# A post-norm trunk on one core: which of a norm's eight feature tiles are turned before the next projection, and when its tiles are normalised

## The chip, the cores and the metric

One core of a Trainium2 chip runs the whole program. The metric is the device time of one execution in microseconds (us); the median of three runs is compared with that of another kernel on the same chip. Engines: TensorE (PE; PEld is its weight load), VectorE (DVE), ScalarE (ACT), GpSimd (POOL) and SyncE (SP, which here only starts transfers). Each engine works through its own queue in order and waits on semaphores for the others.

## What is computed

x is 512 rows of 1024 features. The trunk has two layers, all in float32:

```
for layer in range(2):
    mix = _even_mixer(x, ...) if layer % 2 == 0 else _odd_mixer(x, ...)
    x = _layer_norm(ALPHA * x + mix, ln1_g[layer], ln1_b[layer])
    x = _layer_norm(ALPHA * x + _swiglu(x, gate, up, down), ln2_g[layer], ln2_b[layer])
```

The even mixer is one input projection, gated linear attention and windowed softmax attention, and one output projection; the odd one is a gated DeltaNet between two projections. So there are four norms: norm 1 after the even mixer, norm 2 after the first feed-forward part, norm 3 after the odd mixer, norm 4 at the end. Only norms 1 to 3 are followed by another projection.

## The kernel before

**Products.** A float32 product is made of three passes of rounded parts: high x high, low x high and high x low (`mm3`, L1663). Weights come in blocks of 1 MB into two slots of `w_raw`; ACT rounds each half of a block to `w_hi` (`split_to`, L807) and POOL subtracts to get `w_lo` (L681). Activations are kept by feature, `x_hi` and `x_lo`, 8 feature tiles of 128 x 512.

**A norm** sits between two projections. The sublayer's output comes row-wise, four tiles t of 128 rows, in two halves of 512 columns. The last weight block of the second half runs tile by tile (`tm_group` with `in_turn`), so its banks fill one after another. DVE adds each filled bank to `x_tm` (L1237), takes statistics (L1239) and aggregates them (L1219); ACT takes the square root (L841); DVE takes the reciprocal (L1194) and normalises both halves (L1210). `layer_norm` on DVE (L1190) normalises tile t-1 after the aggregate of tile t, and tile 3 last; in norm 4 it normalises tile t directly (L1221).

PE then turns the rows to features: `turn_x` (L1834), 4 row tiles x 8 feature tiles = 32 transposes of 128 x 128, tile by tile, into eight banks `xT`; feature k is complete with row tile 3. `round_x` on ACT (L819) and DVE (L1159) applies scale and bias to each feature and makes `x_hi` and `x_lo`; feature 1 goes by DVE (`f_ab`) and an ACT copy. Then `fm_block` with `fresh` (L1688) runs the next projection's first block, two output banks, as features arrive: two high passes per feature and bank (L1696, L1697), and the pass with `x_lo` (L1709) two features later. It issues features 0 and 1 bank by bank, 48 products in all. ACT queues the split of the block behind that one (both pieces) between `layer_norm` and `round_x`. POOL splits the low part of its first piece once all is normalised, and of its second once the last `x_lo` is there (L778 to L781).

**Banks.** `unit_plan` (L178) lists all uses of the eight PSUM banks in PE's order and hands them out from a ring; the swap at L277 puts feature 1's bank ahead of feature 0's for the next unit.

**Way in.** While the first weights and features land, PE runs 16 products on zeros (L1879). Then `tm_group` of `sq` runs, three passes each; its first product waits for the low parts of weight and feature tile 0, which DVE makes (L1258, L1261) from ACT's high parts (L883, L879).

**Query copies.** In the even mixer PE turns queries and keys, ACT copies the banks to `s_qT` and `s_kT` (L915, L917), and the bank of query tile 0 is the one that the next product, `a2` (L1904), fills. ACT splits the second block of `gv` ahead of these copies (L911).

Of the kernel before, what the change touches and what calls it, by code (L numbers as in the profile page):

```python
# [164 lines left out]

EVEN_FILLERS = [[("gr", t)] for t in range(NT)]
# [11 lines left out]
def unit_plan():  # L178
# [4 lines left out]
    def ln(i):  # L183
        u.extend(("xT", i, k) for k in range(KD))

    def ffn(layer):
        for f in range(0, KF, 2):
            u.extend([("gate", layer, f), ("gate", layer, f + 1), ("up", layer, f), ("up", layer, f + 1)])
        for half in range(2):
            u.extend(("down", layer, half, t) for t in tiles)  # L190
# [18 lines left out]
    for i, n in enumerate(CONV_ORDER):  # L209
        u.append(("conv", n))  # L210
        if i == 1:
            u.append(("ba_fm",))
# [39 lines left out]
    for key in u:  # L252
# [24 lines left out]
        if key[0] == "xT" and key[2] == KD - 1:  # L277
            a = turn % len(ring)
            c = (turn + 1) % len(ring)
            ring[a], ring[c] = ring[c], ring[a]  # L280
# [6 lines left out]
def trunk_kernel(nc, A, out):  # L287
# [8 lines left out]
    with ctx:  # L296
# [202 lines left out]
        def low_weights_all(e, b):  # L499

            low_weights(e, b, len(pieces(b)) - 1)
# [295 lines left out]
        def _(act):  # L797
# [21 lines left out]
            def round_x(i):  # L819
# [7 lines left out]
                for k in range(2, KD):  # L827
# [10 lines left out]
            def layer_norm(i):  # L838
                for t in range(NT):
                    act.wait_ge(s["ln_var"], NT * (i - 1) + t + 1)  # L840
# [70 lines left out]
            split_to(first_block[("gv",)] + 1)  # L911

            for t in range(NT):
                full(act, ("qT", t))
# [64 lines left out]
            layer_norm(1)  # L979
            split_to(first_block[("gate", 0, 0)] + 1)  # L980
            round_x(1)
# [3 lines left out]
            layer_norm(2)  # L985
            split_to(first_block[("conv", KD)] + 1)
# [5 lines left out]
            round_x(2)  # L992
# [137 lines left out]
            layer_norm(3)  # L1130
            split_to(first_block[("gate", 1, 0)] + 1)
            round_x(3)
# [6 lines left out]
        def _(dve):  # L1139
# [50 lines left out]
            def layer_norm(i, group, layer):  # L1190
# [22 lines left out]
                for half in range(2):  # L1213
                    for t in range(NT):
                        if (group, layer, half, t) not in FILLED:
                            add_sublayer(i, group, layer, half, t)
                        if half:
# [3 lines left out]
                            if i == 4:  # L1221
                                normalise(t)
                            elif t:
                                normalise(t - 1)
                if i < 4:
                    normalise(NT - 1)
# [425 lines left out]
        def _(pe):  # L1652
# [35 lines left out]
            def fm_block(b, keys, fresh=None, width=P):  # L1688
# [10 lines left out]
                for k in range(KD) if fresh is not None else ():  # L1699
                    for n in range(len(keys)):  # L1700
                        if k == 0:
                            high(0, n)
                            high(1, n)
                        elif k > 1:
                            high(k, n)
# [530 lines left out]
```

## Time and profile before

| | |
|---|---|
| median of 3 runs | 1243.77 us (1243.36 to 1244.42) |
| the profiled execution, its own time | 1243.55 us |
| its span in the trace | 1241.7 us, so 1.85 us lie around it |
| PE busy | 1227.7 us, 99% |
| DVE, ACT, POOL busy | 436.9, 450.6, 587.9 us |
| granted TensorE clock, mean | 0.998 |

The page says that PE is busy nearly always, so time can come only from work taken off PE or from the few stretches where it waits. The timeline of one engine lists its instructions with the idle time before them and what ended it; the list of waits sums that by line and releaser.

### The profile page before, as it was taken

To read this page: it belongs to the slowest core of one execution; us is meant where nothing else is said; L and a number is where in the kernel's file an instruction comes from. 1 tells how busy PE (TensorE), PEld (TensorE's weight loads), DVE (VectorE), ACT (ScalarE), POOL (GpSimd) and SP (SyncE) were. 2 spreads that over 40 slices of the span, in tenths; PEclk is the share of its full clock that TensorE was granted. 3 is DMA by queue.
4 is the path that set the end of the run, shared out by engine and by line. 5 is a ranking of instruction groups with operands and counts; after the bars stand their busy time and mean duration, and the time that the engine had idled before them with its cause. 6 is when DMAs were issued, how large, how long until landed. Compare 5 with 4: busy or idle time off the path is not lost.

```text
span 1241.7 us, 17153 instructions
## 1 busy us (share of the span) xinstructions
PE 1227.7 (99%) x7112; PEld 1012.4 (82%) x7112; DVE 436.9 (35%) x772; ACT 450.6 (36%) x670; POOL 587.9 (47%) x280
## 2 busy tenths in 40 slices
PE   9999999999999999999999999999999999999997
PEld 7878887888888888887777889888788888888885
DVE  4556526201011100127678845654511111110105
ACT  4167825232223221225544455542532233221211
POOL 4244444943444343445744347444684444435341
PEclk9999999999999999999999999999999999999999
DMA  9321052333322333232353342124233222324231
GB/s 321 96 69 69 3 169 69 102 102 102 99 93 80 98 124 118 102 102 60 92 123 116 91 114 94 27 69 136 68 102 102 92 92 88 102 85 146 75 102 68
DMA packets 106064, 122.96 MB, mean 99 GB/s; under 512 B 18946, under 2 KB 80580, under 8 KB 105988
## 3 DMA queue, kind: packets, MB, share of 16 engines
q1 hardware_dynamic: 98244, 118.56, 29.9%
q10 hardware_dynamic: 7744, 3.32, 1.1%
q8 instruction: 56, 0.92, 0.3%
q14 instruction: 20, 0.16, 0.0%
HBM read 117.93 MB, written 3.70 MB: 98 GB/s over the span
## 4 chain that ended last, share of the span: by engine, by line
PE 95%; DVE 3%; DVEq 0%; ACT 0%; issue 0%; ACTq 0%
PE bank L1665 27%; PE bank L1666 27%; PE bank L1667 27%; PE bank L2088 4%; PE bank L1696 1%; PE bank L1697 1%; PE bank L1709 1%; DVE stats L1239 1%; DVE x_tm L1237 1%; PE bank L1919 1%; PE bank L2197 1%; PE bank L1731 1%; PE bank L2034 1%; PE bank L2180 0%; PE bank L1855 0%; DVE x_tm L1200 0%
## 5 line engine op out<-in xcount | busy, mean ns | idle before, releaser
L681 POOL TENSOR_TENSOR w_lo<-w_raw,w_hi 128x1024 fp32r<-128x1024 f32 (+1 forms) x200 | 470.2, 2373 | 546.9 <-ACT w_hi L816 521.8
L1665 PE MATMUL bank<-x_hi,w_hi 128*128 128x512 f32 x880 | 344.3, 391 | 0.0
L1666 PE MATMUL bank<-x_lo,w_hi 128*128 128x512 f32 x880 | 342.5, 389 | 0.0
L1667 PE MATMUL bank<-x_hi,w_lo 128*128 128x512 f32 x880 | 342.5, 389 | 0.0
L816 ACT ACTIVATE w_hi<-w_raw 128x1024 fp32r<-128x1024 f32 (+1 forms) x200 | 196.4, 1032 | 206.5 <-issue 161.2
L1665 PEld LDWEIGHTS bank<-x_hi,w_hi 128*128 128x128 f32 x880 | 165.2, 188 | 35.4 <-issue 0.8
L1667 PEld LDWEIGHTS bank<-x_hi,w_lo 128*128 128x128 f32 x880 | 165.2, 188 | 34.4
L1666 PEld LDWEIGHTS bank<-x_lo,w_hi 128*128 128x128 f32 x880 | 165.2, 188 | 33.7
L1246 DVE TENSOR_TENSOR f_ab<-bank,f_ab 128x512 f32<-128x512 f32 x44 | 30.4, 692 | 364.7 <-PE bank L1667 364.7
L1667 PE MATMUL bank<-w_hi,h_lo 128*128 128x512 f32 x352 | 136.9, 389 | 0.0
L1665 PE MATMUL bank<-w_hi,h_hi 128*128 128x512 f32 x352 | 136.9, 389 | 0.0
L1666 PE MATMUL bank<-w_lo,h_hi 128*128 128x512 f32 x352 | 136.9, 389 | 0.0
L1665 PE MATMUL bank<-w_hi,x_hi 128*128 128x512 f32 (+1 forms) x288 | 112.2, 390 | 0.0
L1667 PE MATMUL bank<-w_hi,x_lo 128*128 128x512 f32 (+1 forms) x288 | 109.0, 378 | 0.0
L1666 PE MATMUL bank<-w_lo,x_hi 128*128 128x512 f32 (+1 forms) x288 | 108.9, 378 | 0.0
L1237 DVE SCALAR_TENSOR_TENSOR x_tm<-x_tm,bank 128x512 f32<-128x512 f32 x32 | 22.0, 688 | 246.3 <-PE bank L1667 238.7
L864 ACT ACTIVATE h_hi<-f_ab 128x512 fp32r<-128x512 f32 x44 | 27.8, 632 | 187.4 <-DVE f_ab L1246 187.4
L859 ACT ACTIVATE f_ab<-bank 128x512 f32<-128x512 f32 x44 | 26.3, 598 | 144.8 <-PE bank L1667 140.5
L1667 PEld LDWEIGHTS bank<-w_hi,h_lo 128*128 128x128 f32 x352 | 66.1, 188 | 13.8
L1665 PEld LDWEIGHTS bank<-w_hi,h_hi 128*128 128x128 f32 x352 | 66.1, 188 | 13.7
L1666 PEld LDWEIGHTS bank<-w_lo,h_hi 128*128 128x128 f32 x352 | 66.1, 188 | 13.7
L1454 DVE SCALAR_TENSOR_TENSOR KH<-bank,convw,KH 128x511 f32<-128x511 f32 (+2 forms) x72 | 53.9, 749 | 28.8 <-ACT KH L1004 25.9
(291 smaller groups left out, 1252.1 us busy)
## 6 DMA issues: line engine op xcount, KB each, us to landing
w_raw<-ffn_w_gate_dram SPq DMA_DIRECT2D x22, 1024.0 KB, 5.3
w_raw<-ffn_w_up_dram SPq DMA_DIRECT2D x22, 1024.0 KB, 5.3
w_raw<-ffn_w_down_dram SPq DMA_DIRECT2D x20, 1024.0 KB, 5.0
w_raw<-od_w_in_dram SPq DMA_DIRECT2D x16, 1024.0 KB, 5.8
w_raw<-ev_w_in_dram SPq DMA_DIRECT2D x8, 1024.0 KB, 5.6
w_raw<-ev_w_out_dram SPq DMA_DIRECT2D x4, 1024.0 KB, 5.1
w_raw<-od_w_out_dram SPq DMA_DIRECT2D x4, 1024.0 KB, 5.1
x_fm<-x_fm_dram SPq DMA_DIRECT2D x8, 256.0 KB, 6.9
```

What stands on the lines that cost most here:

```text
L681: pool.tensor_tensor(w_lo[:, b % 2, c], w_raw[:, b % 2, c], w_hi[:, b % 2, c].bitcast(F32), ALU.subtract).then_inc(w_lo_ready, 1)
L816: act.activation(w_hi[:, i % 2, c], w_raw[:, i % 2, c], ACT.Copy).then_inc(w_hi_ready, 1)
L859: take(act.activation(f_ab[:, j, :], bank(("gate", layer, f + j))[:, :], ACT.Silu), ("gate", layer, f + j))
L864: act.activation(h_hi[:, f + j, :], f_ab[:, 2 + j, :], ACT.Copy).then_inc(s["h_hi_ready"], 1)
L1237: take(dve.scalar_tensor_tensor(cols, cols, ALPHA, bank(key)[:, :], ALU.mult, ALU.add), key)
L1239: dve.bn_stats(stats[:, t, half, :], cols).then_inc(s["half_stats"], 1)
L1246: take(dve.tensor_tensor(f_ab[:, 2 + f % 2, :], bank(("up", layer, f))[:, :], f_ab[:, f % 2, :], ALU.mult), ("up", layer, f))
L1454: ins = dve.scalar_tensor_tensor(dst, bank(key)[:, 0:SEQ - back], convw[:, tap:tap + 1], dst, ALU.mult, ALU.add)
L1665: pe.matmul(out_ap, st[0], mv_[0], start=start, stop=False)
L1666: pe.matmul(out_ap, st[0], mv_[1], start=False, stop=False)
L1667: return pe.matmul(out_ap, st[1], mv_[0], start=False, stop=stop)
L2088: return pe.matmul(o, a, b_, start=True, stop=True)
```

## The change

- `turn_x` turns features 0 to 5 (`NOW = 6`) of the four row tiles before the projection, and features 6 and 7 behind its third feature, k == 2. The bank plan follows, and the swaps of ring positions go. `fm_block` issues features 0 and 1 like the others, both banks of a feature together.
- DVE normalises each tile right behind its aggregate in all norms.
- ACT splits the first piece of the following block ahead of the square root of tile 3, and its second piece at the end of `round_x` (`split_part`). In norm 2 three transfers that ACT starts, `ba_w`, `o_upto` and `o_negt`, come behind `round_x`.
- Way in: 12 products on zeros, then four high x high products that wait only for the high parts, then the passes with low parts of weight row 0, then the rest.
- ACT splits `gv`'s second block behind the copies of query and key tiles 0 and 1.

```
--- before.py
+++ after.py
@@ -163,6 +163,7 @@
            (1, 1): ("og", 1, 0), (1, 3): ("og", 1, 1), (2, 1): ("og", 1, 2), (2, 3): ("og", 1, 3),
            (3, 1): ("mix", 1, 0, 0), (3, 3): ("mix", 1, 0, 1)}
 
+NOW = 6
 EVEN_FILLERS = [[("gr", t)] for t in range(NT)]
 TAIL_FILLERS = {0: [("mix", 0, 0, 0), ("mix", 0, 0, 1)], 1: [("mix", 1, 0, 2)]}
 LAST_FILLERS = {0: [("mix", 0, 0, 2)], 1: []}
@@ -180,12 +181,15 @@
     u = []
     tiles = range(NT)
 
-    def ln(i):
-        u.extend(("xT", i, k) for k in range(KD))
+    def ln(i, features=range(NOW)):
+        u.extend(("xT", i, k) for k in features)
 
     def ffn(layer):
         for f in range(0, KF, 2):
-            u.extend([("gate", layer, f), ("gate", layer, f + 1), ("up", layer, f), ("up", layer, f + 1)])
+            u.extend([("gate", layer, f), ("gate", layer, f + 1)])
+            if f == 0:
+                ln(2 * layer + 1, range(NOW, KD))
+            u.extend([("up", layer, f), ("up", layer, f + 1)])
         for half in range(2):
             u.extend(("down", layer, half, t) for t in tiles)
 
@@ -209,6 +213,7 @@
     for i, n in enumerate(CONV_ORDER):
         u.append(("conv", n))
         if i == 1:
+            ln(2, range(NOW, KD))
             u.append(("ba_fm",))
         if i == 2:
             u.append(("ba",))
@@ -274,10 +279,6 @@
         else:
             b = ring[turn % len(ring)]
             turn += 1
-        if key[0] == "xT" and key[2] == KD - 1:
-            a = turn % len(ring)
-            c = (turn + 1) % len(ring)
-            ring[a], ring[c] = ring[c], ring[a]
         order[b] = len(slots)
         slots[key] = (b, uses[b])
         uses[b] += 1
@@ -816,7 +817,17 @@
                         act.activation(w_hi[:, i % 2, c], w_raw[:, i % 2, c], ACT.Copy).then_inc(w_hi_ready, 1)
                     split[0] += 1
 
-            def round_x(i):
+            def split_part(b, j):
+
+                assert split[0] == b
+                if j == 0:
+                    act.wait_ge(w_landed[b % 2], 16 * (b // 2 + b % 2))
+                    act.wait_ge(*block_end[b - 2])
+                    low_weights_all(act, b - 2)
+                act.activation(w_hi[:, b % 2, pieces(b)[j]], w_raw[:, b % 2, pieces(b)[j]], ACT.Copy).then_inc(w_hi_ready, 1)
+                split[0] += j
+
+            def round_x(i, b):
 
                 gcol = 32 * ((i + 1) % 2) + 8 * ((i - 1) // 2)
                 full(act, ("xT", i, 0))
@@ -834,9 +845,12 @@
                             low_part_there(act, i, k - 4)
                         take(act.activation(f_ab[:, k % 4, :], bank(("xT", i, k))[:, :], ACT.Identity, scale=scale,
                                             bias=bias), ("xT", i, k))
-
-            def layer_norm(i):
+                split_part(b, 1)
+
+            def layer_norm(i, b=None):
                 for t in range(NT):
+                    if t == NT - 1 and b is not None:
+                        split_part(b, 0)
                     act.wait_ge(s["ln_var"], NT * (i - 1) + t + 1)
                     act.activation(rstd[:, t:t + 1], mv[:, t, 1:2], ACT.Sqrt, bias=eps[:, 0:1])\
                        .then_inc(s["ln_stat"], 1)
@@ -908,9 +922,10 @@
             split_to(first_block[("gv",)])
             full(act, ("ga",))
             take(act.activation(g_ga[:, :], bank(("ga",))[:, :], ACT.Copy), ("ga",))
-            split_to(first_block[("gv",)] + 1)
 
             for t in range(NT):
+                if t == 2:
+                    split_to(first_block[("gv",)] + 1)
                 full(act, ("qT", t))
                 take(act.activation(s_qT[:, :, tile_cols[t]], fm4(("qT", t)), ACT.Copy), ("qT", t))
                 full(act, ("kT", t))
@@ -976,20 +991,18 @@
             split_to(first_block[("mix", 0, 1)])
             full(act, ("mix", 0, 0, NT - 1))
             split_to(first_block[("gate", 0, 0)])
-            layer_norm(1)
-            split_to(first_block[("gate", 0, 0)] + 1)
-            round_x(1)
+            layer_norm(1, first_block[("gate", 0, 0)] + 1)
+            round_x(1, first_block[("gate", 0, 0)] + 1)
 
             ffn(0)
             split_to(first_block[("conv", KD)])
-            layer_norm(2)
-            split_to(first_block[("conv", KD)] + 1)
+            layer_norm(2, first_block[("conv", KD)] + 1)
+            round_x(2, first_block[("conv", KD)] + 1)
 
             act.dma_start(ba_w[:, :, :], A["od_w_in"][0][:, BA0:BA0 + SB].rearrange("(k p) n -> p k n", p=P))\
                .then_inc(s["ba_landed"], 16)
             for dst, c0, n in ((o_upto, 0, P), (o_negt, P, P)):
                 act.dma_start(dst[:, :], A["c_odd"][:, c0:c0 + n]).then_inc(consts, 16)
-            round_x(2)
 
 
             def silu_conv(i):
@@ -1127,9 +1140,8 @@
             split_to(first_block[("mix", 1, 1)])
             full(act, ("mix", 1, 0, NT - 1))
             split_to(first_block[("gate", 1, 0)])
-            layer_norm(3)
-            split_to(first_block[("gate", 1, 0)] + 1)
-            round_x(3)
+            layer_norm(3, first_block[("gate", 1, 0)] + 1)
+            round_x(3, first_block[("gate", 1, 0)] + 1)
             ffn(1)
             split_to(NB - 1)
             layer_norm(4)
@@ -1218,12 +1230,7 @@
                             dve.wait_ge(s["half_stats"], 2 * NT * (i - 1) + NT + t + 1)
                             dve.bn_aggr(mv[:, t, :], stats[:, t, :, :].rearrange("p a b -> p (a b)"))\
                                .then_inc(s["ln_var"], 1)
-                            if i == 4:
-                                normalise(t)
-                            elif t:
-                                normalise(t - 1)
-                if i < 4:
-                    normalise(NT - 1)
+                            normalise(t)
 
             def add_sublayer(i, group, layer, half, t):
 
@@ -1698,11 +1705,9 @@
 
                 for k in range(KD) if fresh is not None else ():
                     for n in range(len(keys)):
-                        if k == 0:
-                            high(0, n)
-                            high(1, n)
-                        elif k > 1:
-                            high(k, n)
+                        high(k, n)
+                    if k == 2:
+                        turn_x(fresh, range(NOW, KD))
                     for kl in [k - 2] * (k > 1) + [KD - 2, KD - 1] * (k == KD - 1):
                         low_part_there(pe, fresh, kl)
                         for n in range(len(keys)):
@@ -1733,7 +1738,7 @@
                                         skip_group_check=True)
                 done(ins, key)
 
-            def tm_group(name, wait_k, src=xcols, kt=KD, in_turn=False, tiles=range(NT), pair_last=False, late=0):
+            def tm_group(name, wait_k, src=xcols, kt=KD, in_turn=False, tiles=range(NT), pair_last=False, late=0, begun=0):
 
 
                 b = first_block[name]
@@ -1759,7 +1764,7 @@
                         for t in tiles:
                             pe.matmul(bank((*name, t))[:, 0:width], src(kk, tile_cols[t])[0], weights(b, kk, 0, width)[1],
                                       start=False, stop=False)
-                    for kk, t in [(kk, t) for kk, t in steps if kk >= late or k0]:
+                    for kk, t in [(kk, t) for kk, t in steps if kk >= max(late, begun) or k0]:
                         if kk > waited:
                             weights_there(b, kk)
                             wait_k(k0 + kk)
@@ -1831,10 +1836,10 @@
                 if (t, place) in FILLERS:
                     tile_of(FILLERS[t, place], k0, k1)
 
-            def turn_x(i):
+            def turn_x(i, features=range(NOW)):
 
                 for t in range(NT):
-                    for k in range(KD):
+                    for k in features:
                         if k % 4 == 0:
                             pe.wait_ge(s["z_norm"], 2 * (NT * (i - 1) + t) + k // 4 + 1)
                         ps = fill(("xT", i, k)) if t == 0 else bank(("xT", i, k))
@@ -1875,9 +1880,18 @@
                              pair_last=(layer, half) == (1, 1))
 
             pe.wait_ge(s["warm_ready"], 1)
-            for _ in range(16):
+            for _ in range(12):
                 pe.matmul(bank(("skv", NT - 1))[:, :], warm[:, 0:P], warm[:, :], start=True, stop=True)
-            tm_group(("sq",), lambda k: low_part_there(pe, 0, k))
+            pe.wait_ge(s["w_first_hi"], 1)
+            pe.wait_ge(s["x_hi_ready"], 1)
+            for t in range(NT):
+                pe.matmul(fill(("sq", t))[:, :], x_hi[:, 0, tile_cols[t]], weights(0, 0, 0, 512)[0], start=True, stop=False)
+            weights_there(0, 0)
+            low_part_there(pe, 0, 0)
+            for t in range(NT):
+                pe.matmul(bank(("sq", t))[:, :], x_lo[:, 0, tile_cols[t]], weights(0, 0, 0, 512)[0], start=False, stop=False)
+                pe.matmul(bank(("sq", t))[:, :], x_hi[:, 0, tile_cols[t]], weights(0, 0, 0, 512)[1], start=False, stop=False)
+            tm_group(("sq",), lambda k: low_part_there(pe, 0, k), begun=1)
             tm_group(("skv",), no_wait)
             pe.wait_ge(s["eye_landed"], 16)
             pe.wait_ge(consts, 16 * N_CONST)
```

## Rows read from the trace of the kernel before

**Rows 1.** The page, busy time of each engine, share of the span, instructions.

```profile
PE 1227.7 (99%) x7112; PEld 1012.4 (82%) x7112; DVE 436.9 (35%) x772; ACT 450.6 (36%) x670; POOL 587.9 (47%) x280
```

**Rows 2.** Waits of PE: waiting line, releaser: us in total, times, longest.

```profile
PE bank L1841 <- DVE x_tm L1210: 1.1, 3, 0.4
PE bank L1696 <- DVE f_ab L1176: 0.7, 2, 0.3
PE bank L1841 <- DVE x_tm L1237: 0.6, 3, 0.2
PE bank L1904 <- ACT s_qT L915: 0.6, 1, 0.6
```

**Rows 3.** Timeline of PE, norm 1: start, duration, line, operation, count, idle before.

```profile
193.73 0.93 PE L1841 MATMUL bank<-eye,x_tm 128*128 128x128 f32 x7
...
196.44 2.23 PE L1841 MATMUL bank<-eye,x_tm 128*128 128x128 f32 x16 [0.38 <-DVE x_tm L1210]
199.00 0.47 PE L1696 MATMUL bank<-x_hi,w_hi 128*128 128x512 f32 x1 [0.34 <-DVE f_ab L1176]
...
208.77 1.52 PE L1709 MATMUL bank<-x_lo,w_hi 128*128 128x512 f32 x6
210.13 0.39 PE L1665 MATMUL bank<-x_hi,w_hi 128*128 128x512 f32 x1
```

**Rows 4.** Timeline of DVE, norm 1.

```profile
185.76 0.69 DVE L1237 SCALAR_TENSOR_TENSOR x_tm<-x_tm,bank 128x512 f32<-128x512 f32 x1 [12.18 <-PE bank L1667]
...
194.11 0.69 DVE L1237 SCALAR_TENSOR_TENSOR x_tm<-x_tm,bank 128x512 f32<-128x512 f32 x1
...
196.95 1.00 DVE L1210 TENSOR_SCALAR x_tm<-x_tm,mv,rstd 128x512 f32<-128x512 f32 x2
198.05 0.81 DVE L1176 TENSOR_SCALAR f_ab<-bank,lnc 128x512 f32<-128x512 f32 x1
```

**Rows 5.** Timeline of ACT, norm 1.

```profile
196.01 1.99 ACT L816 ACTIVATE w_hi<-w_raw 128x1024 fp32r<-128x1024 f32 x2
198.08 0.78 ACT L823 ACTIVATE x_hi<-bank,lnc 128x512 fp32r<-128x512 f32 x1
```

**Rows 6.** Timeline of DVE, norm 4, which normalises each tile at once.

```profile
1219.09 0.69 DVE L1237 SCALAR_TENSOR_TENSOR x_tm<-x_tm,bank 128x512 f32<-128x512 f32 x1 [42.34 <-PE bank L1667]
...
1221.12 0.16 DVE L1194 RECIPROCAL rstd<-rstd 128x1 f32<-128x1 f32 x1 [0.36 <-ACT rstd L841]
1221.32 1.42 DVE L1200 SCALAR_TENSOR_TENSOR x_tm<-x_tm,mv,ln_rows 128x512 f32<-128x512 f32 x2
```

**Rows 7.** Two transposing groups between products in the even mixer, timeline of PE.

```profile
108.58 1.04 PE L1928 MATMUL bank<-eye,s_p 128*128 128x128 f32 x8
109.49 0.66 PE L1855 MATMUL bank<-eye,o_tm 128*128 128x128 f32 x4
```

**Rows 8.** Way in: PE's line 1879 (ns min/median/max, first and last start).

```profile
L1879 PE MATMUL bank<-warm x16: 388/440/796, 1.5 to 6.5; 128*128 128x512 f32 x16
```

**Rows 9.** Way in: timeline of ACT, high part of feature tile 0.

```profile
5.39 0.62 ACT L879 ACTIVATE x_hi<-x_fm 128x512 fp32r<-128x512 f32 x1
```

**Rows 10.** Way in: timeline of DVE, low part of feature tile 0.

```profile
6.13 0.69 DVE L1261 TENSOR_TENSOR x_lo<-x_fm,x_hi 128x512 fp32r<-128x512 f32 x1
```

**Rows 11.** Way in: timeline of PE, first product of sq.

```profile
6.96 0.47 PE L1665 MATMUL bank<-w_hi,x_hi 128*128 128x512 f32 x1
```

**Rows 12.** Query copies: timeline of ACT.

```profile
66.61 2.00 ACT L816 ACTIVATE w_hi<-w_raw 128x1024 fp32r<-128x1024 f32 x2
68.69 0.60 ACT L915 ACTIVATE s_qT<-bank 128x512 f32<-128x512 f32 x1
```

**Rows 13.** Norm 2: last work of round_x on ACT, timeline.

```profile
570.50 0.77 ACT L835 ACTIVATE f_ab<-bank,lnc 128x512 f32<-128x512 f32 x1
```

**Rows 14.** Norm 2: DMA issues, KB and us to landing.

```profile
ba_w<-od_w_in_dram ACTq DMA_DIRECT2D x1, 128.0 KB, 2.7
```

**Rows 15.** Norm 2: timeline of PE, first use of ba_w.

```profile
574.83 1.92 PE L1731 MATMUL bank<-x_hi,ba_w 128*32 128x512 f32 x16
```

More of the change, by code:

```diff
@@ L181, in unit_plan, with ln @@
     tiles = range(NT)
-    def ln(i):
-        u.extend(("xT", i, k) for k in range(KD))
+    def ln(i, features=range(NOW)):
+        u.extend(("xT", i, k) for k in features)
     def ffn(layer):
         for f in range(0, KF, 2):
-            u.extend([("gate", layer, f), ("gate", layer, f + 1), ("up", layer, f), ("up", layer, f + 1)])
+            u.extend([("gate", layer, f), ("gate", layer, f + 1)])
+            if f == 0:
+                ln(2 * layer + 1, range(NOW, KD))
+            u.extend([("up", layer, f), ("up", layer, f + 1)])
         for half in range(2):
@@ L1734, in few_columns, with tm_group @@
                 done(ins, key)
-            def tm_group(name, wait_k, src=xcols, kt=KD, in_turn=False, tiles=range(NT), pair_last=False, late=0):
+            def tm_group(name, wait_k, src=xcols, kt=KD, in_turn=False, tiles=range(NT), pair_last=False, late=0, begun=0):
                 b = first_block[name]
@@ L1761, in tm_group @@
                                       start=False, stop=False)
-                    for kk, t in [(kk, t) for kk, t in steps if kk >= late or k0]:
+                    for kk, t in [(kk, t) for kk, t in steps if kk >= max(late, begun) or k0]:
                         if kk > waited:
@@ L1832, in filler, with turn_x @@
                     tile_of(FILLERS[t, place], k0, k1)
-            def turn_x(i):
+            def turn_x(i, features=range(NOW)):
                 for t in range(NT):
-                    for k in range(KD):
+                    for k in features:
                         if k % 4 == 0:
@@ L1877, in _ @@
             pe.wait_ge(s["warm_ready"], 1)
-            for _ in range(16):
+            for _ in range(12):
                 pe.matmul(bank(("skv", NT - 1))[:, :], warm[:, 0:P], warm[:, :], start=True, stop=True)
-            tm_group(("sq",), lambda k: low_part_there(pe, 0, k))
+            pe.wait_ge(s["w_first_hi"], 1)
+            pe.wait_ge(s["x_hi_ready"], 1)
+            for t in range(NT):
+                pe.matmul(fill(("sq", t))[:, :], x_hi[:, 0, tile_cols[t]], weights(0, 0, 0, 512)[0], start=True, stop=False)
+            weights_there(0, 0)
+            low_part_there(pe, 0, 0)
+            for t in range(NT):
+                pe.matmul(bank(("sq", t))[:, :], x_lo[:, 0, tile_cols[t]], weights(0, 0, 0, 512)[0], start=False, stop=False)
+                pe.matmul(bank(("sq", t))[:, :], x_hi[:, 0, tile_cols[t]], weights(0, 0, 0, 512)[1], start=False, stop=False)
+            tm_group(("sq",), lambda k: low_part_there(pe, 0, k), begun=1)
             tm_group(("skv",), no_wait)
```

54 lines of the change are left out of this document (27 added, 27 removed).

## Prediction

> **What bounds the kernel now.** I read the page first: PE is busy 99% of the span, every other engine half of it or less [rows 1]. So only two things can move the time: work added to or taken from PE, and PE's waits. The list of PE's waits comes next [rows 2]. Two of its lines belong to the transposes of the norms (1.1 and 0.6 us in three norms), one to the first products behind them (0.7 us in two norms, 0.34 in the row of norm 1), and one to the query copies (0.6). That is (1.1 + 0.6) / 3 + 0.34 = 0.9 us of waiting in each of norms 1 to 3 and 0.6 in the even mixer. What the change can remove is therefore about 3 us and a little at the start, and what it adds to PE's path counts in full, because everything behind each norm is PE-bound.
>
> Then the timelines of norm 1, engine by engine [rows 3 to 5]. PE leaves the last sublayer product at 193.73, turns 32 tiles, and begins the projection at 199.00; the 48 products of that first block end at 210.13. Six products take 1.36 us there (208.77 to 210.13), 0.227 each, so 48 need 10.88 and the block's 11.13 hold only 0.25 of waiting. Who ends the wait before 199.00? DVE normalises row tile 3 from 196.95 to 198.05, ACT is busy with a weight split from 196.01 and rounds feature 0 at 198.08 for 0.78, and PE starts 0.14 after that. So PE waits for row tile 3. While it waits it does transposes that cost nothing; the reader should see that 5.3 us of transposes and waits stand before the first product, and that PE isn't what sets their end.
>
> **Tiles normalised at once.** In the kernel before, DVE takes tile t-1 while ACT takes the square root of tile t, so the round trip to ACT is hidden. Norm 4 shows the other order in this same trace [rows 6]: from the add to the start of the normalising 1221.32 - 1219.09 = 2.23 us, with 0.36 idle for ACT's square root in it. From the start of a normalising pair to DVE's next instruction it is 1.10 (196.95 to 198.05) [rows 4]. One row tile thus takes 3.33 us of DVE, in order and with nothing to fill the wait. PE delivers a row tile in 12 products, 2.72 us [rows 3]. DVE falls behind by 0.6 a tile: tile 0 is added at 185.76 as before, tile 3 at 185.76 + 3 x 3.33 = 195.75 in place of 194.11 [rows 4], and its normalising starts at 195.75 + 2.23 = 197.98 in place of 196.95. That is **1.03 us later**, though tiles 0 to 2 are earlier, which nobody needs.
>
> **The split moved.** ACT's first piece (half of 1.99 [rows 5]) now follows the end of PE's last sublayer product at 193.7 or the square root of tile 2, whichever is later, and is done near 195.5. The square root of tile 3 is asked for at about 197.4, so it hides. If the weights landed 2 us late it would cost the excess. The second piece comes behind the last feature; the next block's second half is read some 3 us after the first block ends, and ACT and POOL need 1 and 2.4 us, so I cost it at nothing. What the move gives: feature 0 no longer queues behind the split. Before, half of tile 3 was normalised about 0.6 after 196.95, one transpose takes 0.3 more, and ACT could have begun near 197.85 instead of 198.08.
>
> **First product.** Tile 3's first half is there at 197.98 + 0.6 = 198.58; a transpose 0.3; ACT 0.78; PE 0.14 later [rows 5]: 199.80, against 199.00. So **+0.80** in norm 1. Feature 1 (DVE free at 199.08, 0.81 for f_ab [rows 4], then ACT's copy, no longer than 0.78) is ready near 200.7, when PE has finished the four products of feature 0. It costs at most 0.2.
>
> **Two feature tiles turned later.** Eight transposes leave the stretch where PE waited anyway and enter the stretch where it has no wait to fill. Of the same shape, eight take 0.91 between products (108.58 to 109.49) [rows 7]; the nearest other row gives 2.23 for sixteen, 1.1 for eight, with waits in it [rows 3]. I take **+0.91**. Their banks are those of features 0 and 1, free once DVE has read them near 200.7, and PE gets there at about 202.6, so no wait. The swap of ring positions that falls served a start in feature 1's bank; the two output banks now are those of the last two sublayer tiles, free after DVE's adds, before 197. Cost nothing.
>
> One norm: 0.80 + 0.91 = **1.71**. From below I allow 1.2 (part of the block's 0.25 filled, a shorter chain), from above 2.2 (1.1 for the transposes, the 0.2 for feature 1, a slow first product). Norms 2 and 3 show the same waits in the list [rows 2], so three make 5.13 (3.6 to 6.6).
>
> In norm 2 ba_w now leaves behind round_x. That ends near 570.50 + 0.77 [rows 13] + 1.0 for the delay, the split adds 1.0, the landing 2.7 [rows 14]: 576.0. PE asks at 574.83 [rows 15] + 1.7 = 576.5. Half a microsecond of cover; I cost it at nothing and put the risk (up to 1) into the range.
>
> **Way in.** The sixteen zero products run from 1.5 to 6.75; the last starts at 6.5 [rows 8]. The first real one starts at 6.96, just behind the low part of feature 0, which ends at 6.82 [rows 10, 11]. Without four, at 0.227 each, the warm products end near 5.9. The high part is there at 5.39 + 0.62 = 6.01 [rows 9], so real products start at about 6.14, and after four of them (0.9) the low part has long been there. Everything moves ahead by 6.96 - 6.14 = **0.82** (0 to 0.9: nothing, if a later weight piece of the first blocks takes over).
>
> **Query copies.** The 2.00 us split stands right ahead of the first query copy at 68.69, for which a2 waits 0.61 [rows 2, 12]. Behind two tiles of copies it blocks only banks that the gv products reach 3 us later. **-0.61** (0 to -0.61).
>
> **Sum.** 5.13 - 0.82 - 0.61 = +3.7 us. The span goes from 1241.7 to 1245.4, the profiled execution from 1243.55 to 1247.25; the median of the runs lies 0.22 above that execution, so 1243.77 becomes about **1247.4**. With all bounds: 3.6 - 0.9 - 0.6 = +2.1 and 6.6 - 0 - 0.3 = +6.3, so 1245.9 to 1250.1.
>
> **Rivals.**
> 1. *It does what it is shaped for; faster.* PE's waits in the norms vanish, because feature 0 no longer stands behind the split and the eight transposes fill gaps in the block: 3 x 0.93 + 1.43 = 4.2, 1239.6. For it: the split at 196.01 is really in the way [rows 5]. Against it: only 0.25 of gaps per block, and tile 3 isn't earlier. It decides at the first product of norm 1: at 199.00 - 0.91 = 198.1 or earlier, the norm gains. Chance 0.12.
> 2. *DVE keeps up.* If the round trip of the square root were hidden, tile 3 would be added at 194.11 and normalised 2.23 later, at 196.34; 0.6 ahead and 0.2 by the moved split nearly pay the 0.91. A norm costs 0.1, the whole is -1.1: 1242.7, no difference that can be told. Against it: the 0.36 idle in norm 4 [rows 6]. Chance 0.11.
> 3. *The clock falls.* PE would stand idle about 2.5 us before tile 3, where the longest wait in a norm was 0.4 [rows 2], and four warm products are gone. In the warm-up sixteen products took 5.25 us, against 16 x 0.227 = 3.63 at the 2.4 GHz pace [rows 3, 8]: a restart from 1.2 GHz costs 1.6. Three of them: 1247.4 + 4.9 = 1252.3. Against it: after 5.3 us with no product but transposes and waits, the products at 199.00 went at full pace. Chance 0.07.
>
> The Trainium skill (TensorE: Matmul & The Clock Gate, Part 1: The HAM clock gate) says that a PE found idle is put back to 1.2 GHz, and that page's Part 4, PE-mode transpose, says that transposes don't count as busy in the same way. By these two together the norms of the kernel before should already have lost the clock, and the pace behind 199.00 says that they didn't; the rule speaks against the change, and rival 3 is what it would make of it.
>
> **How the numbers follow.** The forecast case (1245.9 to 1250.1) has 0.70; 0.05 of that ends under 1246.3. I call 0.2%, 2.5 us, the least that a measurement of this kernel tells from no change. Slower by more: 0.65 + 0.07 = 0.72. Within: 0.05 + 0.10 of rival 2 = 0.15. Faster: 0.12 + 0.01 = 0.13. The range takes in the forecast case and rival 2, 1242.5 to 1250.1, and leaves out rivals 1 and 3, 0.19.
>
> **What would show it.** In the trace after: in norms 1 to 3 DVE idles 0.36 before each reciprocal and the adds are 3.3 apart; normalising of tile 3 starts 1.0 later against PE's last sublayer product; PE idles about 2.5 before tile 3's transposes; the first product comes 6.1 behind the last sublayer product, not 5.3; eight transposes of 0.9 stand in the block, which takes 12.0; the first real product is at 6.1; the wait at a2 is gone. Wrong would be the forecast if adds were 2.8 apart, if the block took 11.3 in spite of the transposes, or if products behind the norm were 0.43 apart.

## The result: slower by 0.9%, and the profile after

The changed kernel takes 1255.41 us in the median of four runs (1254.1 to 1256.21), the kernel before 1243.78 on the same chip: a ratio of 1.0092, with a 95% interval of 1.0079 to 1.0105. The forecast was 1247.4 with a range of 1242.5 to 1250.1. Slower was right, the size was not: +11.6 us where +3.7 was forecast. The profiled execution took 1255.61, its span 1253.8 is 12.1 longer than before.

The list of PE's waits of the changed kernel, the counterpart of [rows 2]:

```profile
PE bank L1846 <- DVE x_tm L1222: 9.6, 6, 2.4
PE bank L1884 <- DVE warm L1259: 1.5, 1, 1.5
PE bank L1672 <- POOL w_lo L682: 0.7, 1, 0.7
```

PE now waits 3.2 us a norm for DVE's normalising (line 1222, which was 1210), up to 2.4 at once. The wait at the query copies is gone, and a wait of 0.7 for POOL's low weights has come. The difference between these waits and those of [rows 2] explains some 7 us of 12, so PE must also be slower at work. The timeline of PE in norm 1, against [rows 3]:

```profile
193.22 1.47 PE L1846 MATMUL bank<-eye,x_tm 128*128 128x128 f32 x12
195.46 0.90 PE L1846 MATMUL bank<-eye,x_tm 128*128 128x128 f32 x6 [0.77 <-DVE x_tm L1222]
198.77 0.89 PE L1846 MATMUL bank<-eye,x_tm 128*128 128x128 f32 x6 [2.42 <-DVE x_tm L1222]
200.01 0.47 PE L1703 MATMUL bank<-x_hi,w_hi 128*128 128x512 f32 x1 [0.35 <-issue]
...
201.27 0.63 PE L1703 MATMUL bank<-x_hi,w_hi 128*128 128x512 f32 x1
201.69 0.63 PE L1704 MATMUL bank<-x_hi,w_lo 128*128 128x512 f32 x1
202.12 0.63 PE L1703 MATMUL bank<-x_hi,w_hi 128*128 128x512 f32 x1
...
203.83 0.53 PE L1703 MATMUL bank<-x_hi,w_hi 128*128 128x512 f32 x1
...
204.42 1.04 PE L1846 MATMUL bank<-eye,x_tm 128*128 128x128 f32 x8
205.22 0.71 PE L1714 MATMUL bank<-x_lo,w_hi 128*128 128x512 f32 x2
...
213.47 0.39 PE L1672 MATMUL bank<-x_hi,w_hi 128*128 128x512 f32 x1
```

Read the starts, not only the durations: from 201.27 to 203.83 there are six steps from product to product, 0.427 us each, where they were 0.227 apart before. I call a product slow when the next one starts more than 0.4 behind it: seven in norm 1, nine in norm 2 and nine in norm 3. 512 columns in 0.427 us are 1.2 GHz, the lower of the two levels. The granted clock says the same: in norm 1 it is 1.00 up to 200.5, 0.50 from 201.0 to 204.0 and 1.00 again from 204.5, and its mean over the span is 0.991 against 0.998. What PE did before it: transposes, and idle for 0.77 and 2.42 us. In norm 2 the clock falls earlier, near 566.0 and still inside the wait, so there the transposes of tile 3 are slow too:

```profile
567.20 1.54 PE L1846 MATMUL bank<-eye,x_tm 128*128 128x128 f32 x6 [2.42 <-DVE x_tm L1222]
```

Six take 1.54 where the six at 198.77 took 0.89. This is rival 3.

DVE in norm 1, against [rows 4]:

```profile
185.25 0.69 DVE L1244 SCALAR_TENSOR_TENSOR x_tm<-x_tm,bank 128x512 f32<-128x512 f32 x1 [12.18 <-PE bank L1674]
...
187.27 0.17 DVE L1206 RECIPROCAL rstd<-rstd 128x1 f32<-128x1 f32 x1 [0.36 <-ACT rstd L855]
187.47 1.75 DVE L1222 TENSOR_SCALAR x_tm<-x_tm,mv,rstd 128x512 f32<-128x512 f32 x2
189.32 0.69 DVE L1244 SCALAR_TENSOR_TENSOR x_tm<-x_tm,bank 128x512 f32<-128x512 f32 x1
...
192.63 0.69 DVE L1244 SCALAR_TENSOR_TENSOR x_tm<-x_tm,bank 128x512 f32<-128x512 f32 x1
...
195.95 0.69 DVE L1244 SCALAR_TENSOR_TENSOR x_tm<-x_tm,bank 128x512 f32<-128x512 f32 x1
...
198.17 1.00 DVE L1222 TENSOR_SCALAR x_tm<-x_tm,mv,rstd 128x512 f32<-128x512 f32 x2
```

The adds of tiles 1, 2 and 3 are 3.31 and 3.32 apart, as forecast, with the 0.36 of waiting. But the normalising of tile 0 takes 1.75 and not 1.00. POOL's timeline has the reason to be tested:

```profile
183.72 4.76 POOL L682 TENSOR_TENSOR w_lo<-w_raw,w_hi 128x1024 fp32r<-128x1024 f32 x2 [6.05 <-ACT w_hi L817]
```

POOL ends at 188.48, in the middle of that normalising. In the kernel before, DVE was in tile 0's add and statistics during that time and normalised it later.

A table of the three norms, all from the timelines of PE: from the last sublayer product to the first product of the projection, and the length of its first block of 48 products.

| us | to the first product, norms 1, 2, 3 | first block | sum of both over the norms | slow products in the block |
|---|---|---|---|---|
| before | 5.27, 5.28, 5.27 | 11.13, 11.26, 11.11 | 49.3 | 0 |
| changed | 6.79, 6.95, 6.93 | 13.46, 13.91, 13.86 | 61.9 | 7, 9, 9 |

The norms cost 12.6, and norm 1 begins 0.5 earlier (193.73 to 193.22): together the 12.1 of the span. The stretches between the norms and behind norm 3 are as long as before to within 0.03.

### The profile page after: what moved, and what is told of

Same layout as the page of the kernel before. It is cut to its first block, busy times and chain, and to the rows that moved or that the text cites. A ratio compares the mean times of both kernels' runs of the same rounds, so it can differ in the third digit from the quotient of the medians.

```text
span 1253.8 us, 17146 instructions
## 1 busy us (share of the span) xinstructions
PE 1232.6 (98%) x7108; PEld 1017.4 (81%) x7108; DVE 441.7 (35%) x772; ACT 450.8 (36%) x670; POOL 587.0 (47%) x280
## 3 DMA queue, kind: packets, MB, share of 16 engines
q10 hardware_dynamic: 7744, 3.32, 1.1%
## 4 chain that ended last, share of the span: by engine, by line
PE 93%; DVE 5%; ACT 1%; POOL 1%; DVEq 1%; issue 0%; ACTq 0%
PE bank L1672 26%; PE bank L1673 26%; PE bank L1674 26%; PE bank L2102 3%; PE bank L1703 1%; PE bank L1704 1%; DVE stats L1246 1%; DVE x_tm L1244 1%; PE bank L1714 1%; DVE x_tm L1222 1%; PE bank L1933 1%; PE bank L2211 1%; POOL w_lo L682 1%; PE bank L1736 1%; PE bank L1846 1%; PE bank L2048 0%
## 5 line engine op out<-in xcount | busy, mean ns | idle before, releaser
L817 ACT ACTIVATE w_hi<-w_raw 128x1024 fp32r<-128x1024 f32 x194 | 190.4, 1031 | 206.2 <-issue 160.3
```

The source lines that it names most:

```text
L817: act.activation(w_hi[:, i % 2, c], w_raw[:, i % 2, c], ACT.Copy).then_inc(w_hi_ready, 1)
```

## The experiments

Each is compared with the kernel before on its own chip. Where a run is set against the changed kernel the two stand on different chips; the medians of the kernel before lie within 0.5 of each other on all of them (1243.6 to 1244.07). "Norms" is the sum in the fourth column of the table above.

**a1_lagged**, the changed kernel with DVE's order of before:

```
-                            normalise(t)
+                            if i == 4:
+                                normalise(t)
+                            elif t:
+                                normalise(t - 1)
+                if i < 4:
+                    normalise(NT - 1)
```

> The changed kernel, but DVE normalises tile t-1 behind the aggregate of tile t in norms 1 to 3, as in the kernel before. Theory (each tile normalised at once makes row tile 3 late, PE idles 2.4 us for it, and the clock falls on top): tile 3 is again normalised 3.2 us behind the last sublayer product and not 4.9, no product is issued at the 1.2 GHz pace, and 4.9 us of lateness and 5.0 of slow clock go: 1255.4 falls to about 1245.5. Rival (the two tiles turned later, or the lower clock reached without the long wait, are the cause): slow products stay behind the norms and the time stays above 1250.

1244.56 against 1243.6, ratio 1.0009 (0.9999 to 1.0018); norms 51.1. PE in norm 1:

```profile
193.01 1.47 PE L1851 MATMUL bank<-eye,x_tm 128*128 128x128 f32 x12
195.72 0.89 PE L1851 MATMUL bank<-eye,x_tm 128*128 128x128 f32 x6 [1.24 <-DVE x_tm L1222]
196.83 0.89 PE L1851 MATMUL bank<-eye,x_tm 128*128 128x128 f32 x6 [0.22 <-DVE x_tm L1222]
198.07 0.47 PE L1708 MATMUL bank<-x_hi,w_hi 128*128 128x512 f32 x1 [0.35 <-issue]
```

The long wait is gone, the first product comes 5.06 behind the last one, no product is slow. So the one line on when DVE normalises carries 10.8 of the 11.6 us. The rest of the change, all of it, is worth +1.0, by the interval between -0.1 and +2.2.

**b1_at_once**, the kernel before with that line alone:

```
-                            if i == 4:
-                                normalise(t)
-                            elif t:
-                                normalise(t - 1)
-                if i < 4:
-                    normalise(NT - 1)
+                            normalise(t)
```

> The kernel before, but each tile normalised at once in norms 1 to 3, nothing else. Theory: tile 3 comes 1.7 us later in each norm. 32 transposes instead of 24 stand before the wait, so PE idles less, near 1.9 us. If the clock falls all the same, 5 us of lateness and 5 of clock: 1253; if it holds, 1249. Rival (at once is harmless by itself, since PE has all eight feature tiles to turn): within 1 us of 1243.8.

1251.74, ratio 1.0064 (1.0049 to 1.0079); norms 57.3. That it is harmful alone is shown. The form is another than I had expected:

```profile
194.24 0.93 PE L1836 MATMUL bank<-eye,x_tm 128*128 128x128 f32 x7
197.71 4.60 PE L1836 MATMUL bank<-eye,x_tm 128*128 128x128 f32 x25 [2.55 <-DVE x_tm L1232]
202.65 0.47 PE L1691 MATMUL bank<-x_hi,w_hi 128*128 128x512 f32 x1 [0.34 <-POOL w_lo L681]
```

With eight feature tiles the eighth bank is the one of the last sublayer tile. PE waits for it after seven transposes, until DVE's add of tile 3 (line 1232), which is late now. The other 25 transposes then stand behind the wait and take 4.60, 0.18 each, where sixteen took 2.23 [rows 3]: the slow pace is in the transposes, and is over when the products begin. It is so in norms 1 and 2; in norm 3 the 25 take only 3.20. With six tiles turned first PE doesn't meet this bank: the first product comes 6.8 to 6.95 behind the last one in the changed kernel, and 8.4, 7.9 and 7.6 here. But no slow product is left here, so with the block counted too this kernel's norms are the shorter ones.

**c1_filled**, the changed kernel with nine products in the wait before row tile 3:

```
+                    if t == NT - 1 and features[0] == 0:
...
+                        for _ in range(FILL):
+                            pe.matmul(ps[:, :], w_hi[:, b % 2, 0:P], w_hi[:, b % 2, 0:512], start=True, stop=True)
```

> The changed kernel with nine products (weights by weights, into the first output bank of the next projection, overwritten later) issued by PE before it turns row tile 3; they cost 2.0 us at the full pace and fill most of the 2.4 us wait. Their results are not used. Theory (the idle PE loses its clock): the products behind the norms run at 0.227 us again and the time falls by about 5, to 1250.5. Rival (the slow pace comes from something else, such as the order of the products or the transposes): the slow products stay, the time is 1255 or above.

1250.48, ratio 1.0056 (1.0041 to 1.0071), and 4.9 less than the changed kernel; norms 56.2.

```profile
195.78 2.32 PE L1849 MATMUL bank<-w_hi 128*128 128x512 f32 x9
198.45 0.90 PE L1854 MATMUL bank<-eye,x_tm 128*128 128x128 f32 x6 [0.35 <-DVE x_tm L1223]
199.69 0.47 PE L1704 MATMUL bank<-x_hi,w_hi 128*128 128x512 f32 x1 [0.35 <-issue]
200.00 0.40 PE L1705 MATMUL bank<-x_hi,w_lo 128*128 128x512 f32 x1
200.24 0.39 PE L1704 MATMUL bank<-x_hi,w_hi 128*128 128x512 f32 x1
```

Work whose results nobody uses makes the kernel faster. The first product comes 6.78 behind the last one, as late as in the changed kernel (6.79), but it and those behind it run at 2.4 GHz (granted clock 1.00 through all of norm 1), and the block falls from 13.46 to 11.90. That isolates the clock: 1.6, 1.9 and 1.9 us in the blocks of the three norms, 5.4 in all, with 0.3 more in the transposes of norms 2 and 3. The profiled execution is the fastest of four, which reach from 1249.5 to 1252.5.

**d1_all_before**, the changed kernel with all eight feature tiles turned first:

```
-NOW = 6
+NOW = 8
```

> The changed kernel with all eight feature tiles turned before the projection (NOW = 8), no ring swap. Theory: the eight transposes go back into the wait and give 0.9 a norm, 2.7 in all; PE idles 0.2 to 0.8 less before tile 3, and if that keeps the clock another 5: 1252.7, or 1247.7 with the clock held. Rival (the deferral costs nothing): 1255.

1252.81, ratio 1.0070 (1.0055 to 1.0085), 2.6 less than the changed kernel. The forecast number came out, by another road: the blocks are 11.0 to 11.1 and hold no slow product, but the first product comes 8.7, 8.0 and 9.4 behind the last one, since PE waits 2.54 on the bank of the last tile and turns 25 tiles behind it, in norms 1 and 3 at the slow pace (4.58 and 4.61), in norm 2 in 3.19. A second wait follows:

```profile
PE bank L1703 <- DVE f_ab L1188: 3.3, 3, 1.3
```

The first product goes into the bank of feature 0, which DVE reads only as its second `f_ab`; the ring swap of the kernel before, which this run leaves out, is there to avoid that. This run doesn't isolate the price of the eight transposes; e1_turned_later does.

**e1_turned_later**, the kernel before with the two tiles turned later, and with the bank plan and the order of products that belong to it. The core of the edit:

```
-                        if k == 0:
-                            high(0, n)
-                            high(1, n)
-                        elif k > 1:
-                            high(k, n)
+                        high(k, n)
+                    if k == 2:
+                        turn_x(fresh, range(NOW, KD))
```

> The kernel before with two feature tiles turned behind the third feature, the bank plan and the order of the products of the changed kernel, and nothing else: DVE lags as before, ACT's split stays in front of round_x. Theory: eight transposes cost 0.8 each norm and nothing comes back, because feature 0 still waits for the split: +2.4, 1246.0. Rival (the transposes were what PE waited on, so the first product comes earlier by as much): 1243.6.

1245.62, ratio 1.0016 (1.0007 to 1.0026), +2.0; norms 51.5, 2.2 more than before. The first product comes 5.24 behind the last one and not 5.27, the blocks take 11.87 to 12.01. Turning them later gives 0.03 and costs 0.8 a norm.

**f1_split_moved**, the kernel before with ACT's split in its new places, in each of the three norms; here the calls of norm 1:

```
-            layer_norm(1)
-            split_to(first_block[("gate", 0, 0)] + 1)
-            round_x(1)
+            layer_norm(1, first_block[("gate", 0, 0)] + 1)
+            round_x(1, first_block[("gate", 0, 0)] + 1)
```

> The kernel before with ACT's split of the following block moved (first piece ahead of the square root of tile 3, second behind round_x), nothing else. Theory: feature 0 is rounded 0.2 earlier, but feature 1 hangs on DVE, which is free at the same time as before: the first product comes up to 0.3 earlier and the fourth at the same time, so no more than 0.5 in all: 1243.1 to 1243.6. Rival (the split is what holds the norms, 0.3 to 0.5 each): 1242.3.

1244.05 against 1243.62, ratio 1.0002 (0.9992 to 1.0011); to the first product 5.28, 5.27 and 5.28. Nothing, and the trace says why:

```profile
198.68 0.47 PE L1706 MATMUL bank<-x_hi,w_hi 128*128 128x512 f32 x1 [0.34 <-DVE f_ab L1186]
```

ACT does round feature 0 earlier, 4.19 behind the last sublayer product and no longer 4.35. But by the ring swap the first product goes into the bank of feature 1, and that is free only when DVE's `f_ab` has read it, at 198.53. DVE is no earlier than before. With the two tiles turned later the first product takes another bank and hangs on ACT alone, and there the moved split is worth 0.2 a norm (5.06 in a1_lagged against 5.24 in e1_turned_later).

**l1_pool_held** and **l2_pool_spared** ask why tile 0's normalising is slow. The first is the changed kernel with

```
+                if b in turned:
+                    pool.wait_ge(s["z_norm"], 2 * NT * (turned[b] - 1) + 2)
```

> The changed kernel, but POOL holds the low part of the next projection's first weight block until row tile 0 is normalised. Theory (in the changed kernel POOL's subtraction runs beside DVE's normalising of row tile 0 and stretches it from 1.00 to 1.75 us): tile 0 takes 1.00, tile 3 comes 0.75 earlier, 2.3 us less in all, near 1253, and less again if the clock falls for less time. Rival (the first tile is slow for a reason of DVE's own): 1.75 stays and the time is 1255.

1258.18, ratio 1.0115 (1.0100 to 1.0130): 2.8 slower than the changed kernel, where 2.3 faster was expected. The timelines of DVE and of POOL say why:

```profile
187.03 1.01 DVE L1224 TENSOR_SCALAR x_tm<-x_tm,mv,rstd 128x512 f32<-128x512 f32 x2
188.13 0.69 DVE L1246 SCALAR_TENSOR_TENSOR x_tm<-x_tm,bank 128x512 f32<-128x512 f32 x1
...
190.35 3.08 DVE L1224 TENSOR_SCALAR x_tm<-x_tm,mv,rstd 128x512 f32<-128x512 f32 x2
...
195.74 1.00 DVE L1224 TENSOR_SCALAR x_tm<-x_tm,mv,rstd 128x512 f32<-128x512 f32 x2
```
```profile
188.12 5.03 POOL L682 TENSOR_TENSOR w_lo<-w_raw,w_hi 128x1024 fp32r<-128x1024 f32 x2 [10.89 <-DVE x_tm L1224]
```

Tile 0 takes 1.01 as the theory has it, but POOL's work only moved onto tile 1. Its normalising starts at 190.35, beside POOL, and ends at 193.43, just behind POOL's end at 193.15. This is no slowing by a factor: DVE's instruction waits until POOL is through. Nor does it strike every instruction of DVE: the add at 188.13 stands beside the same POOL work and takes its usual 0.69. The Trainium skill (GPSIMD Engine Reference, Specifications) says that GpSimd shares its interfaces to the on-chip memory with VectorE, and that this collides with VectorE's instructions in a mode that uses two ports, or with two inputs from that memory. The rows of this run agree that some instructions collide; which of the two cases the normalising is, they don't show.

The trace of the kernel before had already held such a row, in the even mixer. These are DVE and POOL there:

```profile
90.06 2.38 DVE L1329 TENSOR_SCALAR neg_sinks<-sinks 128x8 f32<-128x8 f32 x1
89.91 9.69 POOL L681 TENSOR_TENSOR w_lo<-w_raw,w_hi 128x1024 fp32r<-128x1024 f32 x4 [16.38 <-ACT w_hi L816]
```

Eight elements per row took 2.38 us beside POOL. Where POOL is idle, in j1_start_query_pool below (92.83 in DVE's timeline), the same instruction takes 0.16.

The second is the changed kernel with 8 columns of each of those pieces:

```
+                        c = slice(c.start, c.start + 8)
```

> The changed kernel, but POOL makes only 8 columns of each piece of the low part of the first weight block behind norms 1 to 3, so that it is idle while DVE normalises row tile 0. Left out: the rest of those low parts (the stale ones of an earlier block are used). Theory (a POOL subtraction in flight holds up DVE's normalising, in the changed kernel by 0.75 us at tile 0, in l1_pool_held by 2.1 at tile 1): all four tiles take 1.00, tile 3 comes 0.75 earlier in each norm, 2.3 us less, and a little more if the clock falls for less time: 1252.5 to 1253.1. Rival (holding POOL back changes something else, as the slower l1_pool_held would have it): 1255 or above.

1250.57, ratio 1.0057 (1.0044 to 1.0071), 4.8 less than the changed kernel. The normalising of tile 0 takes 1.00 (187.86 in DVE's timeline), the first product comes 6.19, 6.04 and 6.05 behind the last one in place of 6.79, 6.95 and 6.93. That is 2.4 of the 4.8, as expected. The rest is the clock, of which I had expected a little: 3, 7 and 0 products are slow, not 7, 9 and 9. The wait before tile 3 is still 2.42 long in all three norms. In norm 1 the clock has fallen by the end of the wait, so that the slow stretch covers the transposes of tile 3 (1.54) and is over after three products; in norm 3 it doesn't fall at all (granted clock 1.00 throughout). So the length of the wait alone doesn't settle whether the clock falls and when; what does stays open.

**g1_way_in** and **h1_query_copies** are the kernel before with the new way in alone, and with the moved query split alone. The core of the first:

```
-            for _ in range(16):
+            for _ in range(12):
...
+            for t in range(NT):
+                pe.matmul(fill(("sq", t))[:, :], x_hi[:, 0, tile_cols[t]], weights(0, 0, 0, 512)[0], start=True, stop=False)
...
+            tm_group(("sq",), lambda k: low_part_there(pe, 0, k), begun=1)
```

> The kernel before with the new way in alone (12 products on zeros, four high products first). Theory: real products start 0.5 to 0.8 earlier, by the moment at which the clock reaches 2.4 GHz; from there to the gate projection it holds, and part is given back at POOL's low part of the gate block: 0.3 to 0.6 us, 1243.0 to 1243.3. Rival (four warm products fewer leave the clock at 1.2 GHz for longer, which eats the gain): 1243.6 or above.

1242.82 against 1243.65, ratio 0.9993 (0.9984 to 1.0002), -0.8. It leans the way of the theory, and the interval holds no change too. The edit of the second:

```
-            split_to(first_block[("gv",)] + 1)
...
+                if t == 2:
+                    split_to(first_block[("gv",)] + 1)
```

> The kernel before with the split of gv's second block behind the copies of query and key tiles 0 and 1, nothing else. Theory: 0.6 us is won at a2 and most of it is given back 27 us later, where PE waits for POOL's low part of the second gate block (0.7 us in the changed kernel, and nearly due in the kernel before): between 0 and 0.4 us at the end, 1243.3. Rival (nothing is waiting there when only one of the two gains is made): the whole 0.6 arrives, 1243.0.

1243.86, ratio 1.0001 (0.9992 to 1.0010): nothing. Its list of PE's waits has the wait at a2 exchanged for another of the same size:

```profile
PE bank L1666 <- POOL w_lo L681: 0.7, 1, 0.7
```

PE gets to the second weight block of the gate projection earlier, and POOL's low part of it comes when it came before.

**j1_start_query_pool** tried to bring POOL forward. It has the edits of g1_way_in and h1_query_copies, and ACT splits both blocks of the `gr` projection earlier; norms as before.

```
+            split_to(first_block[("gr",)])
             act.wait_ge(s["k_decayed"], 1)
             act.activation(s_p[:, 0, :, :], g_B[:, :, :], ACT.Exp, scale=-1.0 / TAU).then_inc(s["g_exp"], 1)
-            split_to(first_block[("gr",)])
+            split_to(first_block[("gr",)] + 1)
...
-            split_to(first_block[("gr",)] + 1)
```

> The kernel before with the new way in, the moved query split, and both blocks of the gate projection split earlier on ACT (the first ahead of the wait for k_decayed, the second ahead of the copies of gv), so that POOL has their low parts in time. Norms as before. Theory: the 1.2 to 1.4 us of the start and the copies are kept, since POOL's low part was what took them back: 1242.3. Rival (another engine takes over between 90 and 160 us): 1243 or above.

1245.01, ratio 1.0016 (1.0007 to 1.0025): the rival. The median hides two groups, six of the eleven runs at 1244.7 to 1245.0 and five at 1246.9 to 1247.3. DVE and PE there:

```profile
86.26 3.31 DVE L1323 TENSOR_TENSOR g_kd<-g_k,s_p 128x1024 f32<-128x1024 f32 x1
```
```profile
PE bank L1973 <- ACT g_v L934: 2.9, 1, 2.9
```

Two things went wrong. POOL's earlier subtraction fell onto DVE's multiplication of g_kd, which took 3.31 and not the 1.23 of both kernels; and ACT's copies of gv, now behind the second split, hold a bank that PE needs, for 2.9.

**n1_start_query_gate_later** also has the edits of g1_way_in and h1_query_copies. It leaves the splits of `gr` where they were and gives PE other work first:

```
-                tile_of(gr, 3, 8 if t else 6)
+                tile_of(gr, 3, 8 if t else 4)
...
-                    tile_of(gr, 6, 8)
+                    tile_of(gr, 4, 8)
```

> The kernel before with the new way in, the moved query split, and PE taking features 4 to 7 of the first gate tile (gr, 0) behind the chunk states instead of features 4 and 5 ahead of them, so that it doesn't wait for POOL's low part of gr's second block. Norms as before. Theory: the 0.7 us wait goes, and the 1.2 to 1.4 us of start and copies arrive at norm 1: 1242.3. Rival (the chunk states then wait for their own copies, or the start gives nothing because the clock comes up later): 1243 or above.

1241.8 against 1244.07, ratio 0.9983 (0.9974 to 0.9992). It is faster than both kernels. Its list of waits has neither the wait at a2 nor the one for POOL, and norm 1 begins at 192.01 against 193.73, 1.7 earlier:

```profile
PE bank L1880 <- DVE warm L1253: 1.5, 1, 1.5
PE bank L1842 <- DVE x_tm L1211: 1.1, 3, 0.4
PE bank L1697 <- ACT x_hi L823: 1.0, 3, 0.3
PE bank L1842 <- DVE x_tm L1238: 0.6, 3, 0.2
```

## Why the prediction was wrong, step by step

- **What bounds it.** Right. All that was added to PE's path counted: between the norms the two traces agree to 0.01 (348.16 and 348.17 us from the end of norm 1's block to the last product before norm 2; 293.12 and 293.11 from norm 2 to norm 3, so `ba_w` behind `round_x` cost nothing either).
- **Tiles normalised at once, +1.03 at tile 3.** The mechanism was right, and a1_lagged shows that this line is the harm. The size was not: the step from add to add was 3.31 as worked out, but tile 0 took 0.75 more beside POOL, so tile 3's normalising came 1.73 later. I had taken the 1.00 from an instruction that stood where POOL was idle [rows 4], and did not look at POOL's timeline for the new place. The sum had nothing for this.
- **First product +0.80.** Measured 1.52, 1.67 and 1.66: the 0.80, the 0.75 of POOL, and 0.1 for transposes at the lower clock in norms 2 and 3.
- **Two feature tiles turned later, +0.91.** Measured without the clock in c1_filled: 11.90, 11.99 and 11.93 against 11.13, 11.26 and 11.11, so 0.8, 0.7 and 0.8.
- **The clock.** This is the step that failed. The sum holds nothing for it; the text named it as rival 3, priced it at 4.9 and gave it 0.07; c1_filled puts it at 5.4 in the blocks, and with the clock held that kernel takes 1250.48. The argument against it, that the products at 199.00 ran at full pace behind 5.3 us of transposes, compared unlike stretches: there PE idled 0.2 and 0.4 at a time between transposes [rows 2, 3], here 0.8 and 2.4. An idle 1.24 still kept the clock (a1_lagged, e1_turned_later); 2.42 lost it in all three norms of the changed kernel, though not in norm 3 of l2_pool_spared. The forecast's own timeline contained the idle 2.5 us, and no row of the trace showed such a wait with the clock surviving it. A case that the forecast itself creates and no row speaks on deserved a far larger chance.
- **The split moved, nothing.** Right as a cost. The prediction let the first product of the kernel before hang on ACT's rounding of feature 0; it was held at the same moment by DVE's `f_ab` [rows 3], which is why the move alone gives nothing back (f1_split_moved).
- **Way in -0.82, query copies -0.61.** At the gv projection the profile was 1.44 ahead (70.83 to 69.39), as summed. At norm 1 only 0.5 was left. Of the query's 0.6 nothing arrives by itself (h1_query_copies), because POOL's low part of the gate block is due there; the forecast took "PE-bound everywhere behind" too far and had looked at PE's waits only, where a resource that is just in time doesn't appear. n1_start_query_gate_later gets both gains through.
- **The bounds.** The text gives the query copies 0 to -0.61 and says that the risk of `ba_w`, up to 1, is in the range. The sum of the upper bound uses 0.3 for the first and has no term for the second; with both as stated it would end at 1251.4, and the measured 1255.4 lies outside that too.

The sum with measured terms, against +3.7: 5.7 for the clock (5.4 in the blocks and 0.3 in the transposes), 2.25 for POOL beside tile 0 in three norms and 0.9 lost between start and norm 1 are 8.85 more; the transposes turned later cost 0.4 less. That is 12.15, and the span grew by 12.1.

## What to carry to other kernels

- If a change makes an engine wait where it only ever paused briefly, price the pace of what follows as well as the wait, and check by filling the wait with idle work whether the pace comes back.
- A software lag of one step (normalise tile t-1 while tile t's square root is under way) is not slack to be tidied up: it hides a round trip to another engine. Removing it makes early tiles earlier, which nobody asked for, and the last one later.
- Before an instruction of DVE is moved in time, look at what POOL does at the new place, and look in the trace for instructions that take longer than their size explains: they show which kinds collide.
- A list of an engine's waits shows who is late, not who is barely in time. Before counting a gain upstream as a gain at the end, look for the producer with the least lead behind it, and reorder the consumer's work rather than push the producer onto its neighbours.

## What the runs showed of the hardware that I had not expected

- A POOL subtraction of 128 x 1024 (2.4 us) held up a DVE instruction until POOL was done: a normalising pair of 1.00 took 1.75 or 3.08, by how much of POOL's work was left, and a multiplication of 1.23 took 3.31. An instruction on 128 x 8 took 2.38 beside POOL and 0.16 without, while DVE's adds kept their 0.69.
- The products on zeros at the start ran into the higher clock at moments that differ between executions: sixteen of them were busy for 5.48 us in the kernel before, 6.13 in h1_query_copies, 6.31 in b1_at_once and 6.46 in e1_turned_later. One profile's start can be most of a microsecond off by that alone.
